# Gate one-hots: GpSimd makes the scaled rows of two of four tokens, VectorE compares against a row in PSUM

## What is computed

```python
idx = jnp.take_along_axis(cand_i.reshape(...), best_j, axis=-1)      # first * 128 + second index
gate = jax.nn.softmax(best_s, axis=-1)
act = jax.nn.gelu(jnp.einsum('td,thkd->thk', tb, expert_u[idx]), approximate=False)
w = (gate * act).astype(tb.dtype)
return jnp.einsum('thk,thkd->td', w, expert_v[idx])
```

## Time and profile before

| | us |
|---|---|
| median of 3 runs | 3479.8 (3477.73 to 3480.97) |
| the profiled execution, own time | 3480.5 |
| its span, first to last instruction | 3478.7 |
| mean granted TensorE clock | 0.935 |
| busy: PE / DVE / ACT / POOL | 3023.6 / 2252.1 / 1402.5 / 168.7 |
| gates stage of layer 0, first compare to last copy-out | 883.37 to 1016.96 |
| gates stage of layer 1, first compare to last copy-out | 2644.50 to 2732.37 |

### The profile page before, as it was taken

The page is one execution under the profiler, slowest core; times in us unless marked ns, Lnnn a source line. Parts: engine busy times, 40 slices in busy tenths (PEclk is TensorE's granted clock), DMA queues, the critical chain, the costliest instruction groups (busy, mean ns, idle before and its releaser), DMA issues.

```text
span 3478.7 us, 46396 instructions
## 1 busy us (share of the span) xinstructions
PE 3023.6 (87%) x16447; PEld 2459.2 (71%) x16447; DVE 2252.1 (65%) x4277; ACT 1402.5 (40%) x2304; POOL 168.7 (5%) x146
## 2 busy tenths in 40 slices
PE   6999879744689999999999998876844899999998
PEld 2855434533679898898999996665734788888886
DVE  1346331779987777777777773564289776767665
ACT  2122120211884444444444432222115766666664
POOL 0000000011001111111111110000001000000000
PEclk7899989866899999999999998988977999999999
DMA  9122112514237877778777762232320255555553
GB/s 368 46 91 83 63 36 85 216 50 169 97 115 260 278 261 276 275 259 284 252 253 253 253 240 76 82 103 70 133 85 0 82 184 192 182 192 183 190 186 140
DMA packets 118328, 577.83 MB, mean 166 GB/s; under 512 B 10465, under 2 KB 44385, under 8 KB 54497
## 3 DMA queue, kind: packets, MB, share of 16 engines
q1 hardware_dynamic: 98656, 434.10, 35.0%
q0 software_dynamic: 19584, 142.62, 11.9%
HBM read 556.88 MB, written 19.79 MB: 166 GB/s over the span
## 4 chain that ended last, share of the span: by engine, by line
PE 74%; DVE 13%; ACT 7%; DMA 3%; issue 2%; SPq 0%; DVEq 0%; ACTq 0%
PE ps L592 73%; ACT hot L1264 3%; DMA ring<-in_experts 2%; DVE eq L1708 1%; DMA ring<-in_w_mod 1%; ACT gateB L1250 1%; DVE topi L1669 1%; DVE topi L1677 1%; DVE eq L1717 1%; DVE sc L1671 1%; ACT spill L1256 1%; ACT gateA L1253 1%; DVE top L1666 1%; DVE top L1674 1%; PE ps L691 0%
## 5 line engine op out<-in xcount | busy, mean ns | idle before, releaser
L592 PE MATMUL ps<-h2a,ehi 128*128 128x384 f32 x2048 | 522.6, 336 | 4.4 <-DVE elo L1767 4.4
L1767 DVE TENSOR_TENSOR elo<-ring,ehi 128x1024 fp32r<-128x1024 f32 x256 | 312.6, 1222 | 114.4 <-ACT ehi L1277 114.4
L1800 DVE TENSOR_TENSOR elo<-ring,ehi 128x1024 fp32r<-128x1024 f32 x256 | 312.9, 1222 | 110.9 <-ACT ehi L1299 110.9
L592 PEld LDWEIGHTS ps<-h2a,ehi 128*128 128x128 f32 x2048 | 372.8, 188 | 16.1 <-DVE elo L1767 6.1
L592 PE MATMUL ps<-h2b,ehi 128*128 128x512 f32 x1024 | 365.8, 398 | 0.0
L1299 ACT ACTIVATE ehi<-ring 128x1024 fp32r<-128x1024 f32 x256 | 269.7, 1053 | 210.5 <-PE ps L592 210.1
L592 PE MATMUL ps<-h2a,elo 128*128 128x384 f32 x1024 | 343.8, 336 | 0.0
L1277 ACT ACTIVATE ehi<-ring 128x1024 fp32r<-128x1024 f32 x256 | 271.3, 1061 | 168.4 <-DMA ring<-in_experts 167.4
L592 PE MATMUL ps<-hT,ring 128*128 128x512 f32 (+1 forms) x896 | 307.7, 503 | 0.0
L592 PE MATMUL ps<-h2b,elo 128*128 128x256 f32 x1024 | 287.2, 281 | 0.0
L592 PEld LDWEIGHTS ps<-hT,ring 128*128 128x128 f32 x896 | 168.8, 190 | 126.3 <-issue 115.8
(11 more groups left out here) (314 smaller groups left out, 5007.2 us busy)
## 6 DMA issues: line engine op xcount, KB each, us to landing
ring<-in_experts SPq DMA_DIRECT2D x256, 1024.0 KB, 4.8
ring<-in_w_mod SPq DMA_DIRECT2D x48, 1024.0 KB, 7.7
ring<-in_w_side SPq DMA_DIRECT2D x24, 1024.0 KB, 4.9
ring<-in_w_front SPq DMA_DIRECT2D x12, 1024.0 KB, 4.9
ring<-in_w_merge SPq DMA_DIRECT2D x16, 768.0 KB, 4.3
ring<-in_w_q SPq DMA_DIRECT2D x12, 1024.0 KB, 5.0
gate_scratch<-spill SPq DMA_DIRECT2D x48, 256.0 KB, 2.0
gateA<-gate_scratch SPq DMA_DIRECT2D x4, 3072.0 KB, 20.4
```

What stands on the lines that cost most here:

```text
L592: return pe.matmul(out, w, x, start=start, stop=stop, **k)
L1767: v.tensor_tensor(elo[:, r, 0:DM], ring[:, r, 0:DM], ehi[:, k % 2, :].bitcast(F32), ALU.subtract).then_inc(ulo_ready, 1)
L1800: v.tensor_tensor(elo[:, r, DM:2 * DM], ring[:, r, DM:2 * DM], ehi[:, 2 + b, :].bitcast(F32), ALU.subtract).then_inc(vlo_ready, 1)
```

## The change

In the gates stage:

- DVE's compare with second indices covers tokens 0 and 1 (128x256), its compare-and-multiply of token 3 is gone, and both compares read the row of column numbers from PSUM bank 0 in place of SBUF.
- ACT first waits for `pick_col` and copies `iota` into PSUM bank 0 (new semaphore `iota_ready`, for which DVE waits once in each layer); it scales two one-hots of a group, not three.
- POOL makes the scaled one-hots of tokens 2 and 3, each by one 128x128 compare-and-multiply that reads `iota` from SBUF (new semaphore `hot_pool`, once a group); before each group it waits until PE is done with group n - 4.
- PE waits for `hot_pool` too.
- POOL's first two gathers of layer 0 keep their waits and now stand at the head of its gates stage.

```diff
+            def gather(k):
+                pool.indirect_dma_start(gbuf[:, k % 2, :], None, a["expert_rows"],
+                                        bass.IndirectOffsetOnAxis(gidx[:, k:k + 1], 0)).then_inc(gather_in[k % 2], 16)
...
+                elif kind == "gates":
+                    gb = groups_before(st)
+                    idxT = peer_tiles(l)[1]
+                    pool.wait_ge(pick_col, routes_by(l))
+                    if l < DEPTH - 1:
+                        pool.wait_ge(gidx_ready, 1)
+                        for k in range(2):
+                            gather(k)
+                    pool.wait_ge(x_held, 16 * (l + 1))
+                    for n in range(dense_tokens(l) // 4):
+                        count(pool, gate_ps, gb + n - 3)
+                        for t in (2, 3):
+                            k = 4 * n + t
+                            last = pool.tensor_scalar(hot[:, n % 4, 1, t, :], iota, idxT[:, 1, k:k + 1], idxT[:, 2, k:k + 1],
+                                                      ALU.is_equal, ALU.mult)
+                        last.then_inc(hot_pool, 1)
...
+                            pe.wait_ge(hot_pool, i * 4 + (gb + g + 1))
...
+                    act.wait_ge(pick_col, routes_by(l))
+                    act.activation(ps[:, 0, 0:P], iota, ACT.Copy).then_inc(iota_ready, 1)
                     for n in range(ng):
                         act.wait_ge(hot_eq, gb + n + 1)
-                        for t in range(3):
+                        for t in range(2):
...
+                    dve.wait_ge(iota_ready, l + 1)
+                    row = ps[:, 0, 0:P].unsqueeze(1)
                     for n in range(dense_tokens(l) // 4):
-                        g, k = n % 4, 4 * n + 3
+                        g = n % 4
 
                         count(dve, gate_ps, gb + n - 3)
-                        v.tensor_tensor(hot[:, g, 1, 0:3, :], iota.unsqueeze(1).to_broadcast([P, 3, P]),
-                                        idxT[:, 1, 4 * n:4 * n + 3].unsqueeze(2).to_broadcast([P, 3, P]), ALU.is_equal
+                        v.tensor_tensor(hot[:, g, 1, 0:2, :], row.to_broadcast([P, 2, P]),
+                                        idxT[:, 1, 4 * n:4 * n + 2].unsqueeze(2).to_broadcast([P, 2, P]), ALU.is_equal
                                         ).then_inc(hot_eq, 1)
-                        v.tensor_scalar(hot[:, g, 1, 3, :], iota, idxT[:, 1, k:k + 1], idxT[:, 2, k:k + 1],
-                                        ALU.is_equal, ALU.mult)
-                        v.tensor_tensor(hot[:, g, 0, :, :], iota.unsqueeze(1).to_broadcast([P, 4, P]),
+                        v.tensor_tensor(hot[:, g, 0, :, :], row.to_broadcast([P, 4, P]),
                                         idxT[:, 0, 4 * n:4 * n + 4].unsqueeze(2).to_broadcast([P, 4, P]), ALU.is_equal
                                         ).then_inc(hot_ready, 1)
```

More of the change, by code:

```diff
@@ L376, in build_program @@
             sem("exp_in"), sem("exp_out"), sem("pick_ready"), sem("pick_ps"), sem("pick_col"))
-        hot_eq, hot_times = sem("hot_eq"), sem("hot_times")
+        hot_eq, hot_times, hot_pool, iota_ready = sem("hot_eq"), sem("hot_times"), sem("hot_pool"), sem("iota_ready")
         hot_ready, gate_ps, gate_ready = sem("hot_ready"), sem("gate_ps"), sem("gate_ready")
@@ L566, in _ @@
                         pool.tensor_tensor(e4, e4, t4, ALU.mult).then_inc(eq_times, 1)
+                elif kind == "gates":
[14 more added lines that the diff above has]
+                        last.then_inc(hot_pool, 1)
                 elif kind == "experts":
                     if l < DEPTH - 1:
[L570 to L577, removed]
+                        for k in range(2, NK):
+                            pool.wait_ge(acc_done, k - 1)
+                            gather(k)
                     lo_, up_ = slice(0, KD // 2), slice(KD // 2, KD)
```

## The result

The changed kernel takes 3517.09 us (median of 4 runs, 3514.51 to 3519.66) against 3480.39 us for the kernel before on the same chip: ratio 1.0105, 95% interval 1.0088 to 1.0123, some 37 us slower. I had forecast 3439. The profiled execution spans 3517.9 us, 39.2 more than before.

What follows compares the result with a forecast made beforehand. ACT and VectorE were taken to bind the gates stages together. Layer 0 was to save 26.7 less 3.2 for its start, 23.5 us, and layer 1 17.4: together 40.9, from 3479.8 to 3439 us; range 3428 to 3475.

Steps and rivals of the forecast that it cites:

- What bounds before: Gates stages: ACT at 2.70 us and VectorE at 2.68 us a pair of groups bind together; TensorE waits.
- ACT and VectorE after: Gates stages: a pair of groups falls to 2.12 us (layer 1: 2.07) on ACT and 1.92 us on VectorE.
- The PSUM row at no cost: VectorE's compares in the gates stages: reading the column-number row from PSUM instead of SBUF costs zero more.
- The rule with 120 cycles against 58: VectorE's compares: fixed cost of a PSUM source against SBUF, 0.065 us more an operation; the forecast did not use it.
- GpSimd, the failed step: Gates stages: each 128x128 compare-and-multiply on GpSimd taken as 0.40 us, four a pair 1.60 us, hidden under ACT.
- The prediction's other estimate for these columns: GpSimd's 128 elements at 1.8 cycles each and 1.2 GHz, from the Trainium skill: 0.19 us; not used in the sum.
- The point from which GpSimd binds: Gates stages: GpSimd stays hidden under ACT's 2.12 us a pair while its instruction's pitch is under 0.53 us.
- the point of balance: Gates stages: pitch of GpSimd's instruction at which the change neither gains nor loses, 0.66 us.
- Rival (b): Both gates stages: GpSimd's compare-and-multiply makes the kernel slower; 3523 us at 0.80 us each, 3577 at 0.97; chance 0.12.
- x: Pitch of one GpSimd 128x128 compare-and-multiply in the gates stages; bounds 0.10 and 0.97 us, taken as 0.40.
- rival (c): Gates stages: GpSimd and VectorE still lock each other out despite the PSUM row; 67 us more, 3547; chance 0.05.
- The start of layer 0: Layer 0's gates stage: GpSimd's one-hots wait behind its second gather, so the first copy-out comes 3.2 us later.

Runs made afterwards that it cites:

- e8: Changed kernel, but in even groups VectorE compares all four tokens and GpSimd only multiplies two; layer 0's gathers stand behind GpSimd's fourth group; 3441.47 us, ratio 0.9892.
- e2: Kernel before plus only the PSUM copy of the column-number row, read by VectorE's two large compares; no GpSimd work in the stage; 3481.33 us, ratio 1.0004.
- e4: Changed kernel, but GpSimd makes one scaled one-hot of four and VectorE makes one by compare-and-multiply from PSUM; 3465.41 us, ratio 0.9959.
- e1: Kernel before with a list of GpSimd instructions put at its very start, where GpSimd is idle, to price them; one run, 3478.04 us.
- e5: Changed kernel, but GpSimd's compare-and-multiply covers only columns 0 to 63, the others set to zero once a layer; 3448.0 us, ratio 0.9911.
- e3: Changed kernel, but VectorE's compares read the row of column numbers from SBUF again; 3594.48 us, ratio 1.0328.

## Why the prediction was wrong

**What bounds before**, right: ACT and VectorE together, at 2.70 and 2.68 us a pair. e8, whose pair takes the 2.12 us of the forecast, gains 39 us where the forecast had 41; VectorE has more work in it than the forecast gave it, and the gathers stand elsewhere, so the closeness of the two totals is in part luck. One reading was wrong, though nothing in the sum hangs on it: the gates stages are not the one place where TensorE does not set the pace. The same chain has VectorE's lines of route (L1708, L1669, L1677 and more) at 1% each. And the earlier trace rows shows the clock of layer 0 alone; that of layer 1 reached 1.00 some 6 us after the stage's first product, at 2652 us.

**ACT and VectorE after**, right: 0.97 + 4 x 0.29 on ACT, 0.34 and 0.60 on VectorE, seen as work between waits, and as the pace of e8.

**The PSUM row at no cost**, right, by the row that I chose and by e2. The rule with 120 cycles against 58 (the Trainium skill, VectorE: DVE Perf Modes, the section on the TRN2 errata) would by estimate have made e2 slower by 18 us; the ratio was 1.0004 and at most 1.0013, under 5 us. For the small compare-and-multiply, though, 0.06 us did show in e4, close to the 0.065 of the same rule. Only one width was run, so whether it is a fixed cost or a cost by the column is not known.

**GpSimd, the failed step.** "I take 0.27 + 0.1 = 0.37, rounded up to 0.40 us, since the multiply is the nearest in kind": it is 0.774. Two terms of this were too small. The fixed part was taken from a memset of one column, 0.10 us; it is 0.36 for this instruction (e1). The part by the column was taken from a multiply, 2.1 ns; a compare followed by a multiply has 3.3, so 128 columns take 0.42 us and not 0.27. The prediction's other estimate for these columns, 0.19 us, was still farther off. A two-input multiply of 128 columns does cost 0.41: the number was right for another instruction. The point from which GpSimd binds, 0.53, and the point of balance, 0.66, fit the runs: at 0.56 (e5) GpSimd binds and the kernel is faster than before, at 0.774 it is slower.

**Rival (b)** was the one that came true, with 0.12 of the chance. Its formula at x = 0.774 gives 46 x 0.40 + 4 + 30 x 0.45 = 36 us; the two stages grew by 34. The bounds that I gave x, 0.10 and 0.97, held it, but the range of the time, up to 3475, did not follow them: it stopped at x = 0.64, though no row held x below that. With bounds that wide on the one new instruction, 0.17 for slower was too little.

**The lock**, rival (c), fell in the changed kernel, where each of VectorE's compares has one SBUF input. With two (e3) the engines do hinder each other, at half of what strict turns would cost.

**The start of layer 0**: the first copy-out was to come 3.2 us later, and with the dearer instruction 3.9. Measured from the copy of `idxA` it is 894.78 - 886.12 = 8.66 us against 888.89 - 882.80 = 6.09, 2.6 later. The forecast took the gathers' end from the kernel before, 887.41 - 882.80 = 4.61 us after the copy; it is now 888.25 + 0.97 - 886.12 = 3.10. The second gather's 0.97 us in place of 1.40 is 0.43 of these 1.5 us, the rest lies ahead of its start.

**Left open.** 3.3 us arise ahead of the gates of layer 0, where no instruction of the change runs. TensorE's last 128 records of the merge stage take 58.1 us against 56.9, and the 16 after them 5.42 against 3.73, at a granted clock of 0.94 against 0.97 around them. All seven kernels in which GpSimd works in the gates stage show this in their profiles, and the three in which it does not (before, e1, e2) don't. What links the two was not found. The last 1.7 us of the table go with a lower clock in the final norm, 0.66 for the 10 us from 3499 us where the kernel before had 0.83 at the same place. It does not come with the change as such: e3, e4 and e8 have 0.83 there, e5 has 0.66.

## What to carry to other kernels

An idle engine is a gift only at the price of its own instruction: before work is moved to it, measure that very form (operation, operand kinds, width) in a stretch where the engine has nothing to do; a neighbour in kind can be off by a factor of two. Where several engines work through one buffer in rounds, write each engine's work for a round in one column, and move work until the columns are level; here a pair of layer 0 in steady state cost the largest column to about 0.01 us in every kernel, 3.10, 2.49, 2.40, 2.33, 2.23 and 2.12 us, if no lock stood between two of them. And give the moved part the cheapest form: a two-input multiply of 256 columns behind another engine's compare cost GpSimd 0.61 us a group where compare-and-multiply cost 1.55.

## What the runs showed of the hardware

- GpSimd's compare-and-multiply with two scalars from memory costs 0.36 us and 3.3 ns a column, its plain two-input multiply 0.14 us and 2.1 ns a column (e1). So two inputs were cheaper than one input and two scalars, at 128 columns (0.41 against 0.78 us) and at 512 (1.23 against 2.05).
- Where VectorE and GpSimd contended in e3, it was mainly GpSimd that waited (1.02 us for each instruction of layer 0 in place of 0.77, 47 us in all against VectorE's 8); VectorE's 128x256 grew from 0.42 to at most 0.64 us. In e1, beside GpSimd's wide instructions, a 128x64 operation of VectorE with two SBUF inputs took up to 0.99 us in place of 0.23 when it met the start of one, and 0.22 or 0.23 in the later part of one.
- VectorE's large compares cost the same from PSUM and from SBUF (0.60 and 0.61 us for 128x512), its 128x128 compare-and-multiply costs 0.31 from PSUM (e4) and 0.25 from SBUF.
- In the steady part of the gates stage TensorE's granted clock stayed at 1.00 with waits of 0.42 us before every group (changed kernel), and was between 0.74 and 0.91 in 20 us windows of e3, where the waits were longer (up to 1.8 us).
